# Twelve blocks of the recurrence's output gate, computed for group A only in the shared stage and for group B in its own stage

## The chip, the cores and the metric

The kernel is one launch on one core of one Trainium2 chip. The metric is the device time of that launch in microseconds. All data is fp32, inputs and outputs in HBM.

## What is computed

One decoder layer for 512 prompt tokens and 8 sample tokens. Cut to what matters here:

```
h = rmsnorm(x)
z = h @ w_in              # columns: q 1024, k 1024, v 2048, r 2048, low 16, gu 1024, gv 1024, xq 1024, gates 6144
o = gated linear attention(q, k, v, decay from low)      # 4 heads, d_k 256, d_v 512
branch_a = rmsnorm_per_head(o) * silu(r)                 # r is the recurrence's output gate
branch_b = gMLP spatial gate(gelu(gu), gelu(gv))
branch_c = attention(xq, memory)
merged = g0 * (branch_a @ w_br_gla) + g1 * (branch_b @ w_br_gmlp) + g2 * (branch_c @ w_br_xattn)
x = x + merged @ w_out
x = x + experts(rmsnorm(x))    # product keys, 8 heads, top 16: per token 128 rows of U (dot) and 128 rows of V (sum)
```

## The kernel before, in words

Tokens are split in two groups. **Group A** has prompt tokens 0 to 255 and the 8 samples (264 columns, `WA`), **group B** prompt tokens 256 to 511 (256 columns, `WB`). Features lie on partitions, so a projection is cut in **blocks** of 128 output columns of the weights; a block's weights are one load of 1 MB (`wstream[n]`), and a block is numbered `n` (N_Q, N_K, N_V, N_R, ... are the first blocks of each part of `w_in`; `r` has 16 blocks, N_R to N_R+15).

**The shared stage** (`sp_project`, `act_project`, `dve_project`, `pe_project`) goes through the blocks in order of `n` by the list `PLAIN`, whose last entry is the width: `WA` means that the block is multiplied for A alone, `WZ` for A and B. Here the weights are split on ScalarE (`split_hi`, L531) and VectorE (`split_lo`, L535) in a high and a low part, two slots deep, and each of the 16 pieces of a block is multiplied three times in fp32r (`products`, L551): 48 matmuls of 264 columns for A, 48 more of 256 columns for B. ScalarE evicts with the block's function into `zst2`, SyncE stores the result to `z` (A) and `z_b` (B) in HBM. Before the change all 16 blocks of `r` and all 48 of the gates are `WZ`. Along with the blocks go the samples' steps, at fixed places in `PLAIN`: at N_R ScalarE works out the samples' decay (`act_samples_start`), at N_R+8 PE and ScalarE turn q (`act_samples_q`), and from N_U0 = N_R+12 on each block carries one unit of the samples' state update.

**A's own stages** follow: recurrence, merge of the three branches, w_out, the experts' queries and scores.

**B's passage** (`sp_project_b`, `act_project_b`, `dve_project_b`, `pe_project_b`) then computes the blocks of `PROJECTIONS_B` for B: low, q, k, v, gu, gv, xq, 57 blocks. Weights go to three buffers `raw` in one queue on SyncE (`load_b`, L593; block k+3 is issued when block k is multiplied) and are multiplied unsplit in fp32 (`products_b`, L605, two records a piece, so 32 a block) into two PSUM banks (`bank_b`). ScalarE evicts; most results go through one of four buffers (`z_buffer`, `z_slot`) to `z_b` or `z_late` in HBM. B's recurrence (two chunks of 128 tokens) is woven in: `PE_AT`, `ACT_AT` and `SP_AT` give the passage's block after which an engine does which step, and `dve_project_b` is VectorE's order. Step "r" loads the 16 blocks of `r` from `z_b` into `bra_b`, which VectorE scales by the norm's gain (L1974) and later multiplies by the normalized output (L1947, `o_normed`). Then come `merge_b` for branch a (16 blocks, `bra_b` times w_br_gla), attention, merge for branch c (8 blocks), the spatial gate, merge for branch b (8 blocks), `out_b` (16 blocks of w_out and, after the norm, 16 of the experts' queries, keys and scores) and the **table** stage (`pe_table`, 128 blocks of `peer_u` against B's tokens, L3145). In the merges SyncE's queue alternates weight loads with loads of the gates, and a gate load waits for an eviction by VectorE (`load_gate_b`, L2261).

**The rows.** Beside all of this VectorE works on A's experts: POOL gathers rows (each a 1 MB gather of 128 rows of 8 KB, L2869) into a ring of six, and VectorE takes them one by one: 128 dots with U (L2979), then 128 sums with V (L2984), for two tiles of tokens. The generator `experts_a` holds that order, and `beside(k)` takes k steps of it at fixed places of B's code. It yields ahead of each row, so its call number c works on row c-2. Between rows it also holds the top-16 search of the next tile (`top_head`, eight of them, ahead of V rows 12, 26, 40 ... of the first tile, that is rows 140, 154, 168, 182, 196, 210, 224, 238 over all) and, once the 128 dots are done, `soft_second(0)`, which waits for ScalarE's exponential (`act_soft(0)`); before the change ScalarE does this right after the passage, with the two `act_gelu` of the dots.

## Time and profile before

| what | us |
| --- | --- |
| median of three runs | 4693.71 |
| lowest and highest | 4688.34, 4696.35 |
| span of the profiled execution | 4686.2 |
| PE busy in that span | 4133.9 |
| VectorE busy | 3106.5 |
| GpSimd busy | 1334.0 |
| ScalarE busy | 910.3 |

The profiled execution's own total is not listed beside its span; its span is 7.5 us below the median of the runs and 2.1 us below the lowest, which is what lies around the first and last instruction. PE is TensorE's matmul, PEld its weight load, DVE VectorE, ACT ScalarE, POOL GpSimd, SP SyncE; a name with a q is the engine's issuing side. Stretches are given in us from the start of the span: the shared stage's twelve first blocks of `r` lie at 466.4 to 606.4, B's passage at 1779 to 2281, its merges, attention and spatial gate at 2281 to 2710, `out_b` at 2710 to 2976, the table at 2976 to 3892.

### The profile page before, as it was taken

How to read it: one execution, taken by the hardware profiler on the slowest of the kernel's cores; microseconds unless marked ns; L12 is line 12 of the kernel's file. 1: busy time of each engine (PE TensorE's matmuls, PEld its weight loads, DVE VectorE, ACT ScalarE, POOL GpSimd, SP SyncE). 2: the span in 40 equal slices, each digit the busy share in tenths (PEclk: the TensorE clock that was granted, in tenths of full speed). 3: DMA queues.
4: the chain of work that ended last, by engine and by line, in shares of the span. 5: the costliest groups of instructions: out<-in, count | busy, mean ns of one | idle time of the engine just before them, and what ended most of it. 6: DMA issues, size and time to landing. Idle time of an engine off the chain costs nothing.

```text
span 4686.2 us, 62081 instructions
## 1 busy us (share of the span) xinstructions
PE 4133.9 (88%) x23876; PEld 3601.1 (77%) x23876; DVE 3106.5 (66%) x4549; ACT 910.3 (19%) x1321; POOL 1334.0 (28%) x822
## 2 busy tenths in 40 slices
PE   7999999999898999999876788999999999577555
PEld 7999999999788987887765577887888888344222
DVE  7434134443745656888678876789898457688776
ACT  4334334323432332111000000000000003000100
POOL 0000000000000002444443523444454231466665
PEclk9999999999898999999987798999999999788777
DMA  6555468775354549999999799999999997999998
GB/s 221 199 206 194 146 227 295 284 286 185 117 218 169 211 162 366 417 413 383 418 418 384 312 373 405 423 423 423 418 415 411 404 356 276 413 393 398 422 422 363
DMA packets 304986, 1519.48 MB, mean 324 GB/s; under 512 B 36586, under 2 KB 111802, under 8 KB 138212
## 3 DMA queue, kind: packets, MB, share of 16 engines
q0 software_dynamic: 114288, 830.54, 43.2%
q1 hardware_dynamic: 190500, 686.34, 38.7%
q8 instruction: 119, 1.95, 0.2%
q14 instruction: 79, 0.65, 0.0%
HBM read 1439.05 MB, written 77.71 MB: 324 GB/s over the span
## 4 chain that ended last, share of the span: by engine, by line
PE 59%; DMA 21%; DVE 9%; issue 4%; POOL 3%; DVEq 2%; ACT 2%; ACTq 0%; SPq 0%; POOLq 0%
PE psum L551 30%; PE psum L3145 14%; DMA sb_ring<-in_peer_v,sb_idx_all 8%; PE psum L605 7%; DMA sb_raw<-in_wstream 6%; DMA sb_ring<-in_peer_u,sb_idx_all 3%; POOL sb_ring L2958 2%; PE psum L3401 2%; DVE sb_ring L2979 2%; DVE sb_acc L2984 2%; DMA sb_gt_b<-dram_z_b 1%; PE psum L3383 1%; DVE sb_acc_b L3302 1%; DMA sb_raw_u<-in_wstream 1%; DVEq L2290 1%
## 5 line engine op out<-in xcount | busy, mean ns | idle before, releaser
L551 PE MATMUL psum<-sb_actr,sb_split 128*128 128x264 f32 x8112 | 1005.0, 285 | 27.9 <-DVE sb_actr L2462 12.3
L551 PEld LDWEIGHTS psum<-sb_actr,sb_split 128*128 128x128 f32 x8112 | 993.4, 189 | 33.0 <-issue 22.8
L535 DVE TENSOR_TENSOR sb_split<-sb_raw,sb_split 128x2048 fp32r<-128x2048 f32 x201 | 460.4, 2291 | 698.7 <-ACT sb_split L531 697.7
L2869 POOL DMA_INDIRECT sb_ring<-in_peer_u,sb_idx_all x256 | 421.9, 1648 | 1141.8 <-DVEq L3013 567.0
L2979 DVE CUSTOM_DVE_ANT_0 sb_ring<-sb_ring,sb_htok 128x2048 f32<-128x2048 f32 x264 | 595.4, 2289 | 140.5 <-DMA sb_ring<-in_peer_u,sb_idx_all 134.1
L2984 DVE SCALAR_TENSOR_TENSOR sb_acc<-sb_ring,sb_coef,sb_acc 128x2048 f32<-128x2048 f32 x256 | 601.5, 2350 | 106.5 <-DMA sb_ring<-in_peer_v,sb_idx_all 90.5
L2869 POOL DMA_INDIRECT sb_ring<-in_peer_v,sb_idx_all x256 | 444.6, 1737 | 648.9 <-DVE sb_acc L2984 556.6
L3401 PE MATMUL psum<-sb_ring,sb_diag 128*128 128x512 f32 x512 | 352.8, 853 | 233.2 <-DMA sb_ring<-in_peer_v,sb_idx_all 226.1
L3302 DVE SCALAR_TENSOR_TENSOR sb_acc_b<-sb_ring,sb_coef_b,sb_acc_b 128x2048 f32<-128x2048 f32 x192 | 451.2, 2350 | 131.6 <-DMA sb_ring<-in_peer_v,sb_idx_all 118.5
L2958 POOL DMA_INDIRECT sb_ring<-in_peer_v,sb_idx_all x256 | 435.5, 1701 | 270.2 <-DVE sb_acc_b L3302 132.3
L3401 PEld LDWEIGHTS psum<-sb_ring,sb_diag 128*128 128x128 f32 x512 | 135.3, 277 | 435.0 <-DMA sb_ring<-in_peer_v,sb_idx_all 259.4
L3145 PE MATMUL psum<-sb_h2b,sb_raw_u 128*128 128x256 f32 x2048 | 451.4, 380 | 11.7 <-DMA sb_raw_u<-in_wstream 9.7
L3145 PE MATMUL psum<-sb_h2b,sb_raw 128*128 128x256 f32 x2048 | 450.9, 380 | 9.5 <-DMA sb_raw<-in_wstream 9.4
L3145 PEld LDWEIGHTS psum<-sb_h2b,sb_raw_u 128*128 128x128 f32 x2048 | 387.1, 190 | 72.2 <-DMA sb_raw_u<-in_wstream 18.2
L3145 PEld LDWEIGHTS psum<-sb_h2b,sb_raw 128*128 128x128 f32 x2048 | 387.4, 190 | 69.4 <-DMA sb_raw<-in_wstream 17.5
L531 ACT ACTIVATE sb_split<-sb_raw 128x2048 fp32r<-128x2048 f32 x201 | 384.5, 1913 | 205.9 <-PE psum L551 177.5
L605 PE MATMUL psum<-sb_hxb,sb_raw 128*128 128x256 f32 x1824 | 405.2, 384 | 9.8 <-DMA sb_raw<-in_wstream 7.8
L605 PEld LDWEIGHTS psum<-sb_hxb,sb_raw 128*128 128x128 f32 x1824 | 349.5, 193 | 61.6 <-DMA sb_raw<-in_wstream 10.3
L551 PE MATMUL psum<-sb_actb_hi,sb_split 128*128 128x256 f32 x2048 | 369.0, 279 | 0.0
L551 PEld LDWEIGHTS psum<-sb_actb_hi,sb_split 128*128 128x128 f32 x2048 | 316.3, 188 | 0.0
L551 PE MATMUL psum<-sb_actb_lo,sb_split 128*128 128x256 f32 x1024 | 285.8, 279 | 0.0
L1332 POOL TENSOR_TENSOR sb_kd<-sb_bcum_a 128x1024 f32<-128x1024 f32 x1 | 1.9, 1897 | 728.6 <-DVE sb_att_s L866 728.6
(438 smaller groups left out, 4137.0 us busy)
## 6 DMA issues: line engine op xcount, KB each, us to landing
sb_raw<-in_wstream SPq DMA_DIRECT2D x386, 1024.0 KB
sb_raw_u<-in_wstream SPq DMA_DIRECT2D x64, 1024.0 KB, 18.1
sb_states<-in_state SPq DMA_DIRECT2D x32, 512.0 KB, 3.4
sb_states_t<-in_stateT SPq DMA_DIRECT2D x32, 512.0 KB, 4.0
out_gla_s<-sb_states SPq DMA_DIRECT2D x32, 512.0 KB, 3.1
dram_z<-sb_zst SPq DMA_DIRECT2D x121, 132.0 KB
dram_z_b<-sb_zst SPq DMA_DIRECT2D x77, 128.0 KB
sb_vrow<-dram_v SPq DMA_DIRECT2D x8, 1024.0 KB, 5.0
```

The source lines that it names most:

```text
L531: nc.scalar.activation(split[:, slot, 0, :], raw[:, slot, :], ACT.Copy).then_inc(hi_ready, 1)
L535: nc.vector.tensor_tensor(split[:, slot, 1, :], raw[:, slot, :], split[:, slot, 0, :], ALU.subtract).then_inc(lo_ready, 1)
L551: last = nc.tensor.matmul(psum[:, bank, 0:ntok], w[a], acts(b, kt), start=(i == 0 and a == 0 and b == 0), stop=(i == len(kts) - 1 and a == 1))
L605: last = nc.tensor.matmul(bank_b(q), raw[:, k % 3, w0 + i * P:w0 + (i + 1) * P], acts[:, kt, 0:WB], start=(i == 0), stop=(i == len(kts) - 1))
L2290: dve.drain()
L2869: nc.gpsimd.indirect_dma_start(ring[g % RING][:], None, ins[table], bass.IndirectOffsetOnAxis(ap=col, axis=0)) \
L2958: nc.gpsimd.indirect_dma_start(ring_b[slot_b(y, n)][:], None, ins["peer_v"], bass.IndirectOffsetOnAxis(ap=idx_all[:, 3 + y, n:n + 1], axis ...
L2979: nc.vector.tensor_tensor_reduce(u[:], u[:], htok[:], 1.0, 0.0, ALU.mult, ALU.add, out).then_inc(row_used, 1)
L2984: nc.vector.scalar_tensor_tensor(out=a[:], in0=v[:], scalar=c, in1=a[:], op0=ALU.mult, op1=ALU.add).then_inc(row_used, 1)
L3145: last = nc.tensor.matmul(bank_b(OUTS_U + i), raw_u[u_slot(i)][:, kt * P:(kt + 1) * P], h2b[:, kt, :], start=(kt == 0), stop=(kt == KT - 1))
L3302: nc.vector.scalar_tensor_tensor(out=acc_b[y][:], in0=v[:], scalar=coef_b[y][:, n:n + 1], in1=acc_b[y][:], op0=ALU.mult, op1=ALU.add).then ...
L3401: last = nc.tensor.matmul(psum[:, b, :], diag[:, n // PE_EACH % DIAGS, :], v[:, b * 512:(b + 1) * 512], start=(n < PE_EACH), stop=(n >= SL ...
```

## The change

The first twelve blocks of `r` (N_R to N_J-1, N_J = N_R+12) become `WA` in the shared stage. For B they are loaded and multiplied in the passage, at its places 1 to 12, and evicted with Silu straight into `bra_b`; they are neither stored to `z_b` nor loaded back, and step "r" loads only the last four blocks. Buffers and counters of the stores go by `STORED_B`, the passage's blocks without these twelve. `PE_AT`, `ACT_AT` and `SP_AT` move by 12 (ACT's "ahead_eb" by 2), and ScalarE's `act_soft(0)` and both `act_gelu` move from behind the passage to its place 64 of 0 to 68. VectorE's rows move: 26 to 46 ahead of the first products, 5 to 1 ahead of the last norm, 18 to 24 at the end of the passage; in `out_b` 1 a block instead of 1 and 2 in turn (16 for 24), and 22 for 37 behind the norm. The passage takes 153 calls for 131, `out_b` 44 for 67, which leaves the table one more.

```diff
--- before.py
+++ after.py
@@ -67,7 +67,8 @@
 N_OUT = N_BB + 8
 N_WQ = N_OUT + 16
 N_END = N_WQ + 16
-N_U0 = N_R + 12
+N_J = N_R + 12
+N_U0 = N_J
 N_UNITS = N_U0 + 4 * TS
 N_UEND = N_END + NU
 
@@ -85,18 +86,19 @@
 
 
 OUTS_A = outputs_before(N_END)
-PROJECTIONS_B = (N_LOW,) + tuple(range(N_Q, N_LOW)) + tuple(range(N_GU, N_R)) + tuple(range(N_XQ, N_Q))
+STORED_B = (N_LOW,) + tuple(range(N_Q, N_LOW)) + tuple(range(N_GU, N_R)) + tuple(range(N_XQ, N_Q))
+PROJECTIONS_B = STORED_B[:1] + tuple(range(N_R, N_J)) + STORED_B[1:]
 BLOCKS_B = PROJECTIONS_B + tuple(range(N_BA, N_END))
 
 
 def out_b(n):
 
-    return OUTS_A + (PROJECTIONS_B.index(n) if n < N_R else N_R - N_XQ + outputs_before(n) - N_BA)
+    return OUTS_A + (PROJECTIONS_B.index(n) if n < N_J else len(PROJECTIONS_B) + outputs_before(n) - N_BA)
 
 
 def done_b(n):
 
-    return out_b(n) + 1 if n < N_R else out_b(n + 1)
+    return out_b(n) + 1 if n < N_J else out_b(n + 1)
 
 
 OUTS_U = out_b(N_END)
@@ -608,13 +610,13 @@
 
 
         PLAIN = [(N_MEM0, N_XQ, ACT.Copy, MEM), (N_XQ, N_LOW, ACT.Copy, WA), (N_LOW, N_GU, ACT.Copy, WA),
-                 (N_GU, N_GV, ACT.Gelu, WA), (N_GV, N_R, ACT.Gelu, WA), (N_R, N_R + 4, ACT.Silu, WZ), (N_R + 4, N_R + 8, ACT.Silu, WZ), (N_R + 8, N_U0, ACT.Silu, WZ),
+                 (N_GU, N_GV, ACT.Gelu, WA), (N_GV, N_R, ACT.Gelu, WA), (N_R, N_R + 4, ACT.Silu, WA), (N_R + 4, N_R + 8, ACT.Silu, WA), (N_R + 8, N_J, ACT.Silu, WA),
                  (N_U0, N_G, ACT.Silu, WZ),
                  (N_G, N_UNITS - 4, ACT.Sigmoid, WZ), (N_UNITS - 4, N_UNITS, ACT.Sigmoid, WZ),
                  (N_UNITS, N_BA, ACT.Sigmoid, WZ)]
 
 
-        Z_SINGLE = ((N_R + 1) // 2, N_R // 2)
+        Z_SINGLE = ((N_J + 1) // 2, N_J // 2)
 
         def seg_loop(eng, n0, n1, body):
 
@@ -1235,11 +1237,12 @@
                     pe_samples_turn(pe, 0)
                 if n0 == N_R:
                     pe_samples_turn(pe, 1)
-                    pe.wait_ge(act_lo, 12)
                 if n0 == N_R + 8:
                     pe_samples_q(pe)
                 if n0 == N_U0:
                     pe_samples_own(pe)
+                if n0 == N_J:
+                    pe.wait_ge(act_lo, 12)
                 if n0 == N_UNITS:
                     seg_loop(pe, n0, n0 + ATT_MAX, body)
                     pe_samples_scores(pe)
@@ -1255,9 +1258,9 @@
         Z_A = (N_BA + 1 - Z_SINGLE[0], N_BA - 1 - Z_SINGLE[1], 0, 0)
 
         def z_slot(n):
-            return place_b(n) % 4
-
-        Z_B = tuple(Z_A[k] + len(range(k, N_R - N_XQ, 4)) for k in range(4))
+            return STORED_B.index(n) % 4
+
+        Z_B = tuple(Z_A[k] + len(range(k, len(STORED_B), 4)) for k in range(4))
 
         def z_buffer(n):
 
@@ -1265,7 +1268,7 @@
 
         def z_use_b(n):
 
-            return Z_A[z_slot(n)] + place_b(n) // 4 + 1
+            return Z_A[z_slot(n)] + STORED_B.index(n) // 4 + 1
 
         def func_of(n):
 
@@ -1662,13 +1665,13 @@
 
 
 
-        PE_AT = {3: ("up",), 19: ("sub0", 2), 22: ("sub2", 2), 25: ("sub3", 2), 27: ("kd", 2), 33: ("v", 2), 34: ("o", 2),
-                 35: ("kv", 2), 37: ("sums", 2), 40: ("sub0", 3), 42: ("sub2", 3), 44: ("sub3", 3), 45: ("kd_v", 3), 46: ("o", 3),
-                 47: ("kv", 3), 49: ("sums", 3)}
-        ACT_AT = {5: ("gate",), 10: ("ahead_eb", 2), 20: ("sub2", 2), 23: ("sub3", 2), 28: ("kdtok", 2), 31: ("ahead", 3),
-                  33: ("vtok", 2), 36: ("squares_eb", 2), 38: ("root", 2), 41: ("sub2", 3), 43: ("sub3", 3), 45: ("kdtok_vtok", 3),
-                  48: ("squares", 3), 50: ("root", 3)}
-        SP_AT = {1: ("low",), 4: ("r",), 34: ("q",), 36: ("k",), 39: ("v",), 51: ("state",)}
+        PE_AT = {3: ("up",), 31: ("sub0", 2), 34: ("sub2", 2), 37: ("sub3", 2), 39: ("kd", 2), 45: ("v", 2), 46: ("o", 2),
+                 47: ("kv", 2), 49: ("sums", 2), 52: ("sub0", 3), 54: ("sub2", 3), 56: ("sub3", 3), 57: ("kd_v", 3), 58: ("o", 3),
+                 59: ("kv", 3), 61: ("sums", 3)}
+        ACT_AT = {5: ("gate",), 12: ("ahead_eb", 2), 32: ("sub2", 2), 35: ("sub3", 2), 40: ("kdtok", 2), 43: ("ahead", 3),
+                  45: ("vtok", 2), 48: ("squares_eb", 2), 50: ("root", 2), 53: ("sub2", 3), 55: ("sub3", 3), 57: ("kdtok_vtok", 3),
+                  60: ("squares", 3), 62: ("root", 3), 64: ("soft",)}
+        SP_AT = {1: ("low",), 4: ("r",), 46: ("q",), 48: ("k",), 51: ("v",), 63: ("state",)}
 
         def stored_b(sp, n):
 
@@ -1686,7 +1689,7 @@
             if step == "r":
                 for k in (2, 3):
                     load_gate_b(sp, k)
-                sp.dma_start(bra_b[:], z_b[:, N_R:N_G, :]).then_inc(rc_loaded, 16)
+                sp.dma_start(bra_b[:, N_J - N_R:KT, :], z_b[:, N_J:N_G, :]).then_inc(rc_loaded, 16)
             if step == "q":
                 stored_b(sp, 33)
                 sp.wait_ge(sub_ready, 12)
@@ -1709,8 +1712,11 @@
         def sp_project_b(sp):
             for k, n in enumerate(PROJECTIONS_B):
                 load_b(sp, k + 3)
-                sp.wait_ge(evac_done, out_b(n) + 1)
-                if N_Q <= n < N_LOW:
+                if n in STORED_B:
+                    sp.wait_ge(evac_done, out_b(n) + 1)
+                if N_R <= n < N_J:
+                    pass
+                elif N_Q <= n < N_LOW:
                     sp.dma_start(z_late[:, n - N_Q, :], z_buffer(n)[:, CH:WB]).then_inc(z_stored[z_slot(n)], 16)
                 else:
                     sp.dma_start(z_b[:, n, :], z_buffer(n)).then_inc(z_stored[z_slot(n)], 16)
@@ -1842,6 +1848,10 @@
                 act.wait_ge(kv_ready, 8 * c + 8)
                 nc.scalar.activation(vc_b[:].rearrange("p (h j) t -> p h (j t)", h=4), psum[:, 0:4, :],
                                      ACT.Square).then_inc(squares_ready, 1)
+            if step == "soft":
+                act_soft(act, 0)
+                act_gelu(act, 0)
+                act_gelu(act, 1)
             if step == "root":
                 act.wait_ge(root_in, ROOTS_GLA[1] + c + 2)
                 nc.scalar.activation(norm_b[:], norm_b[:], ACT.Sqrt).then_inc(root_out, 1)
@@ -1855,11 +1865,13 @@
         def act_project_b(act):
             for k, n in enumerate(PROJECTIONS_B):
                 act.wait_ge(out_ready, out_b(n) + 1)
-                if z_use_b(n) > 1:
+                if n in STORED_B and z_use_b(n) > 1:
                     act.wait_ge(z_stored[z_slot(n)], 16 * (z_use_b(n) - 1))
                 if N_Q <= n < N_LOW:
                     nc.scalar.activation(chunk_of(n), bank_b(out_b(n))[:, 0:CH], ACT.Copy)
                     nc.scalar.activation(z_buffer(n)[:, CH:WB], bank_b(out_b(n))[:, CH:WB], ACT.Copy).then_inc(evac_done, 1)
+                elif N_R <= n < N_J:
+                    nc.scalar.activation(bra_b[:, n - N_R, :], bank_b(out_b(n)), ACT.Silu).then_inc(evac_done, 1)
                 else:
                     nc.scalar.activation(z_buffer(n), bank_b(out_b(n)), func_of(n)).then_inc(evac_done, 1)
                 if k in ACT_AT:
@@ -1967,9 +1979,10 @@
             sub_exponents(2, 0)
             sub_exponents(2, 1)
             kd_exponents(2)
-            beside(26)
+            beside(46)
             products_ahead(2)
             dve.wait_ge(rc_loaded, 48)
+            dve.wait_ge(evac_done, out_b(N_J - 1) + 1)
             for kt in range(KT):
                 nc.vector.tensor_scalar(bra_b[:, kt, :], bra_b[:, kt, :], pcols[:, C_GLA + kt:C_GLA + kt + 1], None, ALU.mult)
             beside(4)
@@ -1987,9 +2000,9 @@
             scores(3, (2, 2, 2, 2))
             beside(13)
             new_state(3)
-            beside(5)
+            beside(1)
             normed_out(3)
-            beside(18)
+            beside(24)
 
 
 
@@ -2266,7 +2279,7 @@
                 if n == N_BC + 2:
                     sp.dma_start(x1b[:], ins["xbT"]).then_inc(x1_loaded, 16)
                 if n == N_BA:
-                    stored_b(sp, N_R - N_XQ)
+                    stored_b(sp, len(STORED_B))
                     for k in (0, 1):
                         load_gate_b(sp, k)
                 if n == N_BA + 3:
@@ -2709,7 +2722,7 @@
             nc.vector.memset(ssum[:], 0.0)
             dve.drain()
             for n in range(N_OUT, N_WQ):
-                beside(1 + n % 2)
+                beside(1)
                 dve.wait_ge(out_ready, out_b(n + 1))
                 at = x1b[:, n - N_OUT, :]
                 nc.vector.tensor_tensor(at, bank_b(out_b(n)), at, ALU.add).then_inc(evac_done, 1)
@@ -2729,7 +2742,7 @@
                                                       scalar=pcols[:, C_FFN + kt:C_FFN + kt + 1],
                                                       in1=rstd[:, 0:WB], op0=ALU.mult, op1=ALU.mult)
             dve.drain().then_inc(normed, 1)
-            beside(37)
+            beside(22)
 
         def pe_out_b(pe):
             pe.wait_ge(merged_ready, 5)
@@ -3475,9 +3488,6 @@
             act_merge(act, N_BB, N_OUT)
             act_out(act)
             act_project_b(act)
-            act_soft(act, 0)
-            act_gelu(act, 0)
-            act_gelu(act, 1)
             act_attention(act, GB)
             act_spatial(act, GB)
             act_out_b(act)
```

## Rows read from the trace of the kernel before

**Rows 1.** The page: the span, and the busy time of each engine

```profile
span 4686.2 us, 62081 instructions
PE 4133.9 (88%) x23876; PEld 3601.1 (77%) x23876; DVE 3106.5 (66%) x4549; ACT 910.3 (19%) x1321; POOL 1334.0 (28%) x822
```

**Rows 2.** Stretches: length, busy us (instructions) by engine, PE clock, DMA share, GB/s

```profile
466.40:606.40 140.00, 139.31 (x1174) 138.74 (x1172) 28.00 (x15) 42.16 (x48) 0.41 (x2) 1.00 0.41 147
1779.00:2281.00 502.00, 473.19 (x2304) 406.55 (x2304) 400.79 (x585) 69.10 (x137) 200.91 (x126) 0.96 0.99 406
2281.00:2438.00 157.00, 118.43 (x512) 100.41 (x512) 115.52 (x138) 4.73 (x7) 73.79 (x41) 0.87 1.01 418
...
2710.00:2823.00 113.00, 112.12 (x512) 98.09 (x512) 83.12 (x110) 0.00 (x0) 34.54 (x26) 0.99 0.94 371
...
2848.00:2962.00 114.00, 110.60 (x493) 96.28 (x493) 70.46 (x60) 5.75 (x15) 41.05 (x31) 0.96 1.00 412
2976.00:3892.00 916.00, 895.88 (x4101) 775.21 (x4102) 702.00 (x1196) 65.66 (x270) 384.52 (x231) 1.00 1.00 409
```

**Rows 3.** PE in order of time, shared stage: start, us, what, idle before

```profile
385.80 11.87 PE L551 MATMUL psum<-sb_actr,sb_split 128*128 128x264 f32 x96 [1.92 <-ACT sb_zst L1042]
...
478.83 6.06 PE L551 MATMUL psum<-sb_actr,sb_split 128*128 128x264 f32 x48 [0.69 <-DVE sb_split L535]
484.73 0.28 PE L551 MATMUL psum<-sb_actb_hi,sb_split 128*128 128x256 f32 x1
...
490.33 5.97 PE L551 MATMUL psum<-sb_actr,sb_split 128*128 128x264 f32 x48
496.14 0.28 PE L551 MATMUL psum<-sb_actb_hi,sb_split 128*128 128x256 f32 x1
```

**Rows 4.** ScalarE in order of time, at the first block of r

```profile
471.19 1.28 ACT L705 ACT_TABLE_LOAD   x1
472.48 0.26 ACT L705 ACTIVATE sb_es<-sb_gxs 128x64 f32<-128x64 f32 x1
...
474.34 1.92 ACT L531 ACTIVATE sb_split<-sb_raw 128x2048 fp32r<-128x2048 f32 x1
```

**Rows 5.** PE in order of time, B's passage

```profile
1849.30 85.00 PE L605 MATMUL psum<-sb_hxb,sb_raw 128*128 128x256 f32 x384 [5.82 <-DMA sb_raw<-in_wstream]
```

**Rows 6.** DMA issues in B's passage: KB each, median us to landing

```profile
sb_bra_b<-dram_z_b SPq DMA_DIRECT2D x1, 2048.0 KB, 23.7
```

**Rows 7.** VectorE in order of time, end of the passage and first merge

```profile
2240.49 3.35 DVE L1941 RECIPROCAL sb_norm_b<-sb_norm_b 128x512 f32<-128x512 f32 x1 [3.71 <-ACT sb_norm_b L1847]
...
2259.57 2.28 DVE L2979 CUSTOM_DVE_ANT_0 sb_ring<-sb_ring,sb_htok 128x2048 f32<-128x2048 f32 x1
...
2302.31 2.29 DVE L2979 CUSTOM_DVE_ANT_0 sb_ring<-sb_ring,sb_htok 128x2048 f32<-128x2048 f32 x1 [2.32 <-DMA sb_ring<-in_peer_u,sb_idx_all]
...
2315.82 0.41 DVE L2288 TENSOR_TENSOR sb_merged<-psum,sb_gt 128x256 f32<-128x256 f32 x1
```

**Rows 8.** ScalarE in order of time, end of the passage

```profile
2251.94 0.38 ACT L1864 ACTIVATE sb_zst<-psum 128x256 f32<-128x256 f32 x1 [6.52 <-PE psum L605]
...
2282.37 0.31 ACT L2847 ACTIVATE sb_gate_all<-sb_gate_all 128x128 f32<-128x128 f32 x1
```

**Rows 9.** PE in order of time: waits in B's merges, attention and spatial gate

```profile
2328.23 23.88 PE L605 MATMUL psum<-sb_bra_b,sb_raw 128*128 128x256 f32 x96 [16.71 <-DMA sb_raw<-in_wstream]
...
2473.80 1.12 PE L2061 MATMUL psum<-sb_ident,sb_prob 128*128 128x128 f32 x4 [6.66 <-DVE sb_prob L2133]
...
2605.76 0.80 PE L2351 MATMUL psum<-sb_wspat,sb_vn 128*128 128x128 f32 x2 [10.63 <-DVE sb_vn L2420]
```

**Rows 10.** PE's waits from 2847 to 3900: us in total, times, longest

```profile
PE psum L3145 <- DMA sb_raw_u<-in_wstream: 9.7, 20, 1.4
PE psum L3145 <- DMA sb_raw<-in_wstream: 9.4, 19, 1.4
...
PE psum L605 <- DMA sb_raw<-in_wstream: 3.4, 1, 3.4
```

## The prediction

> **What bounds the kernel now.** I read the page first: PE is busy for 4133.9 of 4686.2 us, VectorE for 3106.5 [rows 1]. Such shares mix stages, so next came the stretches [rows 2]. The reader is to see three regimes. In the shared stage at the first twelve blocks of r, PE is busy for 139.31 of 140.00 us while the transfers move only 147 GB/s: PE alone sets the pace. In B's passage both are full: PE 473.19 of 502.00 us, DMA share 0.99. In the first merge PE has 118.43 of 157.00 and the DMA share is 1.01: transfers, and VectorE's place in them, set the pace. From 2710 on PE leads again: 512 records, which are 16 blocks, in 112.12 of 113.00 us, so 7.0 us a block, and the table's 128 blocks take 916, of which 895.88 are PE. The waits of PE in those last stages come to 9.7, 9.4 and 3.4 us [rows 10].
>
> Durations are from the one profiled execution with its span of 4686.2; the median of the runs, 4693.71, is 7.5 higher, and I add my difference to the median.
>
> **What is taken out of the shared stage.** In order of time [rows 3] B's part of a block runs from 484.73 to 490.33, 5.60 us, and A's from 490.33 to 496.14, 5.81. Twelve of B's parts are 67.2 us. Three things give some back, as a block now covers 5.8 us and not 11.4.
> - At the first block of r ScalarE works out the samples' decay, and its split of the second block starts only at 474.34 [rows 4]. It takes 1.92, VectorE's lower part follows, and PE starts at 478.83 after a wait of 0.69 [rows 3]. B's part of the first block hid this: that block's A part ended one B part (5.60) and the wait earlier, at about 472.5. Without the B part PE waits from there to 478.83, 6.4 for 0.69: 5.8 lost.
> - ScalarE changes its function table around the segments' first blocks. In the A-only segment ahead of r such places cost PE up to 1.92 us each [rows 3]. For three segments I take 3.3; bounds 0 and 6.
> - The turning of the samples' q at the ninth block delays the next split. No row of an A-only block has it; between 0 and 2, I take 1.
> VectorE's and SyncE's work per block fits: A-only blocks ran at 5.8 in the stretch before. The stores of z_b that go (twelve of 128 KB) cost nothing at 147 GB/s and bring nothing. Sum: 67.2 - 5.8 - 3.3 - 1 = **57 us gained**, bounds 51 and 62.
> One table load lasts 1.28 us here and the activation behind it starts 0.01 us after [rows 4]. The Trainium skill (ScalarE: Activation LUTs, What ACT_TABLE_LOAD costs) counts a drain of about 1.38 us more per switch, 2.66 together. By that rule some six switches would cost an estimated 8 us more and the gain would be 49; the row speaks for the load alone, and the sum goes by the row.
>
> **What is put into the passage.** 384 records, twelve blocks, took 85.00 us beside full transfers [rows 5]; so the twelve new blocks are 85.0 us of PE. Unsplit fp32 costs 7.08 us a block where the split product cost 5.60: on PE the exchange alone loses 18 us. By bytes: 12 weight loads of 1.049 MB are 12.6 MB, 22 more gathered rows 23.1, and the load of bra_b shrinks from 2048 to 512 KB [rows 6], -1.6. At the 418 GB/s of a full stretch [rows 2] the 34.1 MB take 81.6 us. So both limits grow alike, and 22 rows are about what the time can carry. The smaller bra_b load takes 3.8 us off a crowded moment in which PE waited 5.82 for weights [rows 5]; I take all of it: **81 us lost**, bounds 76 and 88. ScalarE's eviction into bra_b, one piece less on SyncE's queue (no store) and the scaling by VectorE, which waits for an eviction long done, are on no path: the twelve blocks are the first of the passage.
>
> **The backlog at the first merge.** VectorE ends the passage late already: its rows run on to 2302.31 and its first merge eviction is at 2315.82 [rows 7], while PE was done with the passage at 2281; PE waits 16.71 for weights [rows 9] whose issue stands behind that eviction on SyncE's queue. The change adds here. First, six more rows at the end: between 2259.57 and 2302.31 ten rows took 42.7, 4.3 each, so 26 us with weights flowing, or 15 at 418 GB/s once PE stands and they don't. Second, a wait: call 129 now falls inside the last norm, and it ends in soft_second(0), which needs ScalarE's exponential. That moves to place 64, three blocks behind the sums; its eviction is at 2251.94 in the old times, the exponential about 2 us later, where the reciprocal began at 2240.49 [rows 7, 8]. VectorE would stand some 15 us, its ring full and POOL behind it. SyncE, PE and ScalarE go on; PE needs the norm's result only at 2281. Together 30 to 41 us of later rows, cushioned by faster gathers while PE stands, by fuller buffers afterwards, and by the exponential and the gelus that before came at 2282.37. I take **20 us lost**, bounds 0 and 40.
>
> **The searches move.** With 22 more rows behind it, each later stage meets other top-16 searches. By the calls, attention has one before (row 168) and none after; PE waited 6.66 there. The spatial gate has one (196) and none after; PE waited 10.63 [rows 9]. The first merge gets three for two, the second two for one. Attention and spatial gate are chains of small steps, so 7 and 9 are gained; in the merges about 5 are given back: **11 gained**, bounds 0 and 18.
>
> **What out_b and the table gain.** They lose 23 - 1 rows of 1 MB, 23 MB, which would be 55 us by transfers. But PE bounds these blocks at 7.0 us, and all its waits for weights there are 22.5 [rows 10]. VectorE doesn't hold PE up in them. The 6 rows inside the norm stay. I take **6 gained**, bounds 0 and 22. The end of the kernel is untouched.
>
> **Sum:** -57 + 81 + 20 - 11 - 6 = +27, so 4694 + 27 = **4721**. About 0.2% (9.4 us) is what a measurement of this kernel can tell from no change.
>
> **The rivals.**
> - *Bytes set the end of B's part* (faster). If the transfers bound everything from 1779 to 3892, rows taken out of out_b pay for those put into the passage, and only 12.6 - 1.6 = 11.0 MB are new: 26 us. Then -57 + 26 = -31: 4663. It decides if PE's 85 us find idle PE time later. For it: DMA shares of 0.99 to 1.01 from 1779 to 2438, and 1.00 in the table. Against: in the stage that the rows leave, PE is busy 112.12 of 113.00 at 371 GB/s, and nothing there can become shorter.
> The Trainium skill (DMA: Bandwidth & Descriptors, Issuing engines are not separate DMA queues) says that transfers from all issuing engines interleave on the same 16 DMA engines. That rule makes gathers and weights one account, as this rival has it.
> - *A draw.* The backlog is swallowed by buffers and the late stages save most of their waits: -57 + 81 + 3 - 11 - 16 = 0: 4694.
> - *The backlog compounds* (slower still). VectorE comes 40 us late to the first merge, three searches there instead of two add 9, nothing is saved later: -57 + 84 + 40 - 11 - 0 = +56: 4750. It decides if the stand for the exponential and the six rows add up in full at 2281.
> - *The change doesn't do what it says*: compiled code keeps the pace of the shared stage, because ScalarE and VectorE can't follow at 5.8 us. The A-only rows speak against it; then +30 on top.
>
> **Chances.** Forecast with its spread 0.45, compounding 0.15, draw 0.17, bytes 0.20, the last 0.03. Of the forecast's 0.45 some 0.03 falls below no change. Faster by over 0.2%: 0.21; within: 0.15; slower: 0.64. The forecast's own range is 4700 to 4745; the range with the rivals that carry eight in ten is 4668 to 4750.
>
> **What would show it.** In the profile after: the first twelve blocks of r in 80 to 86 us; 12 x 32 more records of L605 and a passage of about 583 us with PE busy near 94%; L2837 in VectorE's waits with some 15 us for ScalarE ahead of L1941; PE's first long wait of the merges longer by some 20; no search inside attention and spatial gate; out_b's 16 blocks still in 112 us, the table in 905 to 916. It is wrong if out_b and table shrink by more than 22 us together, or if the first merge isn't later than the passage's end by more than before.

## The result: 0.74% slower, and the profile after

The kernel after takes 4727.59 us (median of four runs, 4722.02 to 4734.17) where the kernel before took 4695.03 on the same chip: ratio 1.0074, 95% interval [1.0061, 1.0086]. The forecast was 4721, slower, with 4668 to 4750. The profiled execution spans 4720.1 us for 4686.2, +33.9.

The page after, span and busy time (it answers to [rows 1]):

```profile
span 4720.1 us, 61688 instructions
PE 4136.6 (88%) x23684; PEld 3601.0 (76%) x23684; DVE 3106.9 (66%) x4549; ACT 914.8 (19%) x1323; POOL 1332.4 (28%) x822
```

PE's busy time is 2.7 us more than before in total, so nearly all of the 33.9 us that were lost is waiting. The shares show no more; the stretches do (columns as in [rows 2]):

```profile
468.80:550.20 81.40, 74.17 (x596) 73.19 (x594) 28.00 (x15) 39.31 (x37) 0.38 (x2) 0.96 0.62 220
1719.00:2291.00 572.00, 553.06 (x2686) 474.75 (x2687) 431.05 (x608) 79.24 (x155) 208.60 (x139) 0.98 0.98 402
2291.00:2489.00 198.00, 118.63 (x515) 101.33 (x514) 153.70 (x209) 1.67 (x2) 92.84 (x50) 0.80 0.95 388
2749.00:2863.00 114.00, 113.42 (x512) 99.17 (x512) 55.74 (x70) 0.00 (x0) 16.52 (x18) 0.97 0.89 333
3012.00:3926.00 914.00, 897.81 (x4141) 780.81 (x4140) 689.46 (x1184) 70.45 (x275) 389.99 (x225) 1.00 0.97 398
```

The reader is to see one row above all: the first merge, 198 us for the same 118 us of PE work that took 157 before. In `out_b` the transfers fell from 371 to 333 GB/s and the stretch still has its 114 us.

The lengths of the stages, each from PE's first instruction of the stage to its first of the next, in us. For e9 to e12 see the experiments:

| stage | before | after | e9 | e10 | e12 |
| --- | --- | --- | --- | --- | --- |
| shared and A's stages | 1779.3 | 1719.1 | 1789.5 | 1724.7 | 1718.4 |
| B's passage | 501.9 | 572.4 | 563.9 | 563.6 | 569.7 |
| first merge | 157.1 | 198.1 | 197.4 | 159.6 | 136.3 |
| attention | 41.7 | 37.8 | 34.5 | 41.7 | 41.7 |
| second merge | 88.1 | 90.6 | 90.6 | 85.4 | 88.9 |
| spatial gate | 51.6 | 42.3 | 42.3 | 51.6 | 51.6 |
| third merge | 90.0 | 89.3 | 87.9 | 90.7 | 90.1 |
| `out_b`, both halves | 266.5 | 266.9 | 265.1 | 267.9 | 267.6 |
| table | 917.9 | 908.6 | 910.5 | 915.7 | 915.5 |
| end | 792.0 | 795.1 | 791.4 | 788.4 | 792.6 |

PE at the first blocks of r (it answers to [rows 3]): the wait of 6.28 us, where the forecast had 6.4.

```profile
468.83 6.06 PE L553 MATMUL psum<-sb_actr,sb_split 128*128 128x264 f32 x48
481.16 9.01 PE L553 MATMUL psum<-sb_actr,sb_split 128*128 128x264 f32 x57 [6.28 <-DVE sb_split L537]
```

The end of the passage and the first merge of after, in order of time, on VectorE (it answers to [rows 7]):

```profile
2266.14 0.28 DVE L2850 TENSOR_REDUCE sb_sums<-sb_gate_all 128x8 f32<-128x128 f32 x1 [17.72 <-ACT sb_gate_all L2860]
...
2267.16 3.35 DVE L1953 RECIPROCAL sb_norm_b<-sb_norm_b 128x512 f32<-128x512 f32 x1
...
2311.99 0.48 DVE L2789 MAX8 sb_top_v<-sb_sc 128x8 f32<-128x128 f32 x2
...
2321.69 34.27 DVE L2997 SCALAR_TENSOR_TENSOR sb_acc<-sb_ring,sb_coef,sb_acc 128x2048 f32<-128x2048 f32 x14
2355.88 0.41 DVE L2301 TENSOR_TENSOR sb_merged<-psum,sb_gt 128x256 f32<-128x256 f32 x1
2356.22 0.48 DVE L2789 MAX8 sb_top_v<-sb_sc 128x8 f32<-128x128 f32 x2
...
2474.71 0.48 DVE L2789 MAX8 sb_top_v<-sb_sc 128x8 f32<-128x128 f32 x2
...
2489.10 0.42 DVE L2301 TENSOR_TENSOR sb_merged<-psum,sb_gt_b 128x256 f32<-128x256 f32 x1
```

on ScalarE (to [rows 8]):

```profile
2264.03 0.38 ACT L1876 ACTIVATE sb_zst<-psum 128x256 f32<-128x256 f32 x1 [6.52 <-PE psum L607]
2264.43 1.28 ACT L2860 ACT_TABLE_LOAD   x1
2265.73 0.31 ACT L2860 ACTIVATE sb_gate_all<-sb_gate_all 128x128 f32<-128x128 f32 x1
```

on SyncE's queue, where the row of 51.26 us is three loads of gates, the third issued at its end:

```profile
2305.39 51.26 SPq L2274 DMA_DIRECT2D sb_gt<-dram_z_b  x3
2356.70 0.45 SPq L595 DMA_DIRECT2D sb_raw<-in_wstream  x1
```

and on PE (to [rows 9]):

```profile
2291.46 27.79 PE L607 MATMUL psum<-sb_bra_b,sb_raw 128*128 128x256 f32 x128
2367.39 9.87 PE L607 MATMUL psum<-sb_bra_b,sb_raw 128*128 128x256 f32 x32 [48.14 <-DMA sb_raw<-in_wstream]
...
2489.57 6.76 PE L2037 MATMUL psum<-sb_kvt,sb_xq 128*128 128x256 f32 x16 [11.36 <-DVE sb_merged L2301]
```

This is one chain. VectorE stands 17.72 us for the exponential, so the reciprocal starts at 2267.16. The rows behind it, and one top-16 search (the first MAX8, at 2311.99, until the rows go on at 2321.69), run to 2355.88, which is 64.4 us behind PE's first instruction of the merge (34.6 before). SyncE's third gate load waits for that first eviction; the next weight load is issued at 2356.70, the moment it is free, and PE gets it after 48.14 us of waiting. PE's row names the weights, but these were not slow: they landed within 10.7 us of their issue (PE goes on at 2367.39). They were issued late. At the merge's end another search, at 2474.71, stands ahead of the last eviction, and PE waits 11.36 us for it at the start of the attention. Before, that wait was 0.88:

```profile
2438.35 3.72 PE L2024 MATMUL psum<-sb_kvt,sb_xq 128*128 128x256 f32 x16 [0.88 <-DVE sb_merged L2288]
```

The late waits (answer to [rows 10]), PE from 2890 to 3930:

```profile
PE psum L3158 <- DMA sb_raw<-in_wstream: 6.9, 15, 1.4
PE psum L3158 <- DMA sb_raw_u<-in_wstream: 6.1, 13, 1.4
PE psum L607 <- DMA sb_raw<-in_wstream: 4.3, 1, 4.3
```

### The profile page after: what moved, and what is told of

It is laid out like the page before. It is cut to its first block, busy times and chain, and to the rows that moved or that the text cites. A ratio compares the mean times of both kernels' runs of the same rounds, so it can differ in the third digit from the quotient of the medians.

```text
span 4720.1 us, 61688 instructions
## 1 busy us (share of the span) xinstructions
PE 4136.6 (88%) x23684; PEld 3601.0 (76%) x23684; DVE 3106.9 (66%) x4549; ACT 914.8 (19%) x1323; POOL 1332.4 (28%) x822
## 4 chain that ended last, share of the span: by engine, by line
PE 61%; DMA 19%; DVE 9%; issue 5%; POOL 3%; DVEq 2%; ACT 2%; SPq 0%; ACTq 0%; POOLq 0%
PE psum L553 28%; PE psum L3158 15%; PE psum L607 11%; DMA sb_ring<-in_peer_v,sb_idx_all 9%; DMA sb_raw<-in_wstream 8%; DVE sb_acc L2997 2%; POOL sb_ring L2971 2%; DVE sb_acc_b L3315 1%; PE psum L3414 1%; PE psum L3396 1%; DVE sb_ring L2992 1%; DMA sb_raw_u<-in_wstream 1%; DVEq L2303 1%; DVE sb_split L537 1%; POOL sb_ring L2882 1%
## 5 line engine op out<-in xcount | busy, mean ns | idle before, releaser
L2882 POOL DMA_INDIRECT sb_ring<-in_peer_u,sb_idx_all x256 | 393.1, 1536 | 1257.8 <-DVE sb_dots L2992 586.8
L2882 POOL DMA_INDIRECT sb_ring<-in_peer_v,sb_idx_all x256 | 473.8, 1851 | 617.6 <-DVE sb_acc L2997 525.5
L2971 POOL DMA_INDIRECT sb_ring<-in_peer_v,sb_idx_all x256 | 433.5, 1693 | 273.8 <-DVE sb_acc_b L3315 139.1
L607 PE MATMUL psum<-sb_hxb,sb_raw 128*128 128x256 f32 x2208 | 490.5, 383 | 12.6 <-DMA sb_raw<-in_wstream 10.6
L607 PEld LDWEIGHTS psum<-sb_hxb,sb_raw 128*128 128x128 f32 x2208 | 420.9, 192 | 78.3 <-DMA sb_raw<-in_wstream 17.7
L553 PE MATMUL psum<-sb_actb_hi,sb_split 128*128 128x256 f32 x1664 | 299.8, 279 | 0.0
L553 PEld LDWEIGHTS psum<-sb_actb_hi,sb_split 128*128 128x128 f32 x1664 | 257.0, 188 | 0.0
L553 PE MATMUL psum<-sb_actb_lo,sb_split 128*128 128x256 f32 x832 | 232.2, 279 | 0.0
L3114 ACT ACTIVATE sb_a_tile<-psum 128x128 f32<-128x128 f32 x128 | 35.5, 278 | 840.3 <-PE psum L3158 840.3
```

The source lines that it names most:

```text
L553: last = nc.tensor.matmul(psum[:, bank, 0:ntok], w[a], acts(b, kt), start=(i == 0 and a == 0 and b == 0), stop=(i == len(kts) - 1 and a == 1))
L607: last = nc.tensor.matmul(bank_b(q), raw[:, k % 3, w0 + i * P:w0 + (i + 1) * P], acts[:, kt, 0:WB], start=(i == 0), stop=(i == len(kts) - 1))
L2882: nc.gpsimd.indirect_dma_start(ring[g % RING][:], None, ins[table], bass.IndirectOffsetOnAxis(ap=col, axis=0)) \
L2971: nc.gpsimd.indirect_dma_start(ring_b[slot_b(y, n)][:], None, ins["peer_v"], bass.IndirectOffsetOnAxis(ap=idx_all[:, 3 + y, n:n + 1], axis ...
```

## The experiments

Twelve kernels ran; ratios are to the kernel before, run alongside. The theory ("by code") was that the passage pays PE's price for the twelve blocks and that VectorE's lateness at the first merge pays for the rest. Against it stood bytes as one account over all of B's stages.

**e1 to e3: the lateness, piece by piece.**

e1 is the kernel after, with the exponential before the norm's root and the gelus left at place 64:

```diff
-                  60: ("squares", 3), 62: ("root", 3), 64: ("soft",)}
+                  60: ("squares", 3), 61: ("exp",), 62: ("root", 3), 64: ("gelus",)}
...
-            if step == "soft":
+            if step == "exp":
                 act_soft(act, 0)
+            if step == "gelus":
                 act_gelu(act, 0)
```

> The changed kernel, but ScalarE works out the exponential for soft_second(0) at place 61 of the passage; only the two gelus stay at place 64. My theory (VectorE stands 17.7 us inside the last norm for an exponential three blocks too late, and arrives at the first merge that much later): VectorE's wait at the sum of the softmax shrinks to 2 to 5 us, the first merge eviction moves from 64 us behind the passage's end to 50 to 54, and the kernel gains 8 to 16 us against the changed kernel, so 4712 to 4720 where the kernel before is at 4695. Rival (the end of this part is set by the bytes that the transfers have to move, so a stand of VectorE is made good by gathers that land meanwhile): within 4 us of the changed kernel, 4724 to 4731.

4718.25, ratio 1.0063 [1.0050, 1.0076]: about 5 us gained on after by the ratios, so little that the intervals leave it open. By the ratio this is missed: the kernel before ran at 4688.06 beside it and not at 4695, and 1.0063 is where the rival's 4724 to 4731 lay. The merge still took 192.8, and its first eviction came 58.3 us behind PE and not 50 to 54. VectorE's reciprocal starts 14.6 us earlier, but then VectorE stands 5.3 us for the gelus, and 10.7 us for gathers where it had stood 7.6. So taking the stand away brings the eviction 6.1 us forward and not 14.6: the gelus are what VectorE would have waited for next.

e2 is the kernel after, six rows moved from the end of the passage behind the norm:

```diff
-            beside(24)
+            beside(18)
...
-            beside(22)
+            beside(28)
```

> The changed kernel, but 18 rows instead of 24 at the end of the passage and 28 instead of 22 behind the norm of out_b. My theory (the six rows are backlog at the first merge, and out_b and table are bound by PE, so the rows are nearly free there): the first merge eviction comes 14 to 20 us earlier, the merges gain that, out_b and table lose 0 to 3; 4710 to 4716. Rival (bytes set the end of B's part): the same bytes in another order, 4724 to 4731.

4710.75, ratio 1.0046 [1.0032, 1.0060], about 13 us gained, as expected; the merge fell to 169.9. Its first eviction came 14.6 us earlier, which is the time of six rows. The edit does a second thing: no search stands ahead of the merge's last eviction any more, and PE waits 1.22 us there and not 11.36; the attention has one instead (44.5 us for 37.8). The table did not grow (906.8), as the six rows fell in `out_b`, with 56 gathers there for 49.

e3 is the kernel after, twenty rows moved from ahead of the first products behind the norm:

```diff
-            beside(46)
+            beside(26)
...
-            beside(22)
+            beside(42)
```

> The changed kernel, but 26 rows as before instead of 46 ahead of the first products, and 42 instead of 22 behind out_b's norm: the rows' move is undone, the move of the twelve blocks stays. My theory (the passage is bound by PE, with or without the 20 rows; the late stages are bound by PE and have room for some 27 rows): passage 565 to 572 us instead of 572, out_b and table 3 to 8 longer, the searches fall on other stages again (one in attention, one in the spatial gate: 7 and 9 us lost there, some given back in the merges); 4727 to 4742. Rival (bytes set the pace): the passage is 20 x 2.5 = 50 us of transfers lighter and out_b and table 50 us heavier, so the passage drops to PE's 553 and the late stages grow by 30 or more; 4745 to 4760.

4732.10, ratio 1.0092 [1.0078, 1.0106]. The number is inside the first expectation, its terms are not: the first merge fell from 198.1 to 138.2, but the passage grew to 607.0 (565 to 572 expected) and the table by 23 to 931.6 (3 to 8 expected with `out_b`). The passage grew by an accident of the edit. With 20 calls fewer ahead, the dot of row 127 falls behind the norm, and ScalarE, which takes the gelus at place 64, waits 49.67 us for it and evicts nothing. ScalarE of e3 in order of time:

```profile
2316.63 0.26 ACT L2984 ACTIVATE sb_gelus<-sb_dots 128x64 f32<-128x64 f32 x1 [49.67 <-DVEq L3042]
```

and PE of e3, held up by it:

```profile
2317.30 12.93 PE L607 MATMUL psum<-sb_hxb,sb_raw 128*128 128x256 f32 x49 [40.14 <-ACT sb_zst L1876]
```

So e3 says nothing of the rows in the passage. It does show that with twenty calls fewer ahead, place 64 is too early for the gelus.

**e4: PE's work without bytes.** The kernel before, the passage's places 1 to 12 multiplied twice from the same weights.

```diff
-            for i, kt in enumerate(kts):
+            for i, kt in list(enumerate(kts)) * (2 if 1 <= k <= 12 else 1):
```

> The kernel before, but in B's passage the blocks at places 1 to 12 are multiplied twice from the same loaded weights: 84 us more of PE, no byte and no row more. My theory (PE sets the passage, the backlog of VectorE's rows sets the first merge): passage 502 + 84 less 10 to 20 of waits that PE has for VectorE and weights, so 566 to 576; VectorE comes to the passage's end with more rows landed, but its order of rows is fixed, so the first merge stays within 10 us of its 157; total 4755 to 4770. Rival (bytes set the whole of B's part, the transfers are full for most of it): PE's second pass fills time in which the transfers catch up, and later stages get shorter by most of it; total under 4730.

4743.23, ratio 1.0115 [1.0098, 1.0132]; the passage +57.4, the first merge unchanged (155.9). The stretch:

```profile
1780.00:2339.00 559.00, 547.85 (x2688) 475.48 (x2688) 400.95 (x586) 68.89 (x137) 208.07 (x127) 0.98 0.91 365
```

PE work alone lengthens the passage while the transfers relax to 365 GB/s. That is against the bytes rival. But the 384 records more, 79.1 us by their busy time (484.3 for 405.2), made the passage only 57.4 longer: less than the 64 to 74 of the first expectation, and a total between the two. It is the first sign that the passage had idle PE time to give.

**e5 and e6: both repairs, and more of one.** e5 is e1 and e2 together; e6 has `beside(8)` at the end of the passage and `beside(38)` behind the norm.

> The changed kernel with both edits: the exponential at place 61, and 18 rows at the passage's end with 28 behind out_b's norm. My theory (the backlog at the first merge is the sum of the stand for the exponential and of the rows): the two gains of their own runs, 5 and 13 us against the changed kernel, add up, so about 18 less than the changed kernel, ratio to the kernel before 1.0025 to 1.0050; the passage and first merge together 735 to 742 us where the changed kernel has 770. Rival (bytes): no more than the better of the two, ratio 1.0045 or above.

4702.35, ratio 1.0021 [1.0012, 1.0030], some 25 us off after, just more than the first expectation had (1.0025 to 1.0050), and the rival is out; merge 159.8, table 909.5. What happens at the first merge was the change's largest loss, and together the two repairs took no less off than the sum of their own (18). As in e2, a search leaves the merge for the attention with them.

> The changed kernel with the exponential at place 61 and only 8 rows at the passage's end, 38 behind out_b's norm. My theory: the backlog is gone, PE waits at the first merge no longer than its transfers need (50 MB of weights and rows and 4 MB of others at 418 GB/s, some 130 to 140 us for the merge), out_b and table take the rows for 0 to 5 us; 40 to 60 us less than the changed kernel, ratio 0.994 to 0.999. Rival (bytes set the whole of B's part): moved rows bring nothing beyond the stand for the exponential, ratio 1.004 or above.

4701.11, ratio 1.0015 [1.0006, 1.0024]: missed, between the two expectations, with 28 us off after and not 40 to 60. The merge fell further, to 145.4, but against e5 the second merge took 7 more and the table 922.1, 12.6 more, with seven rows more in it.

**e7 and e8: the same on the kernel before.** e7 has 8 for 18 rows at the passage's end and 47 for 37 behind the norm; e8 also 8 fewer in the first merge (`beside(1 + n % 2)` there) and 55.

> The kernel before, its blocks as they are, but with 8 rows instead of 18 at the passage's end and 47 instead of 37 behind out_b's norm. My theory (the backlog was there before the change, smaller): first merge 157 falls to 130 to 138, the spatial gate loses its search (9 us), out_b and table take the ten rows for 0 to 10; ratio 0.991 to 0.996, and 10 to 20 us below the changed kernel with the same treatment (PE: 12 blocks cost 7.0 us in the passage for 5.6 in the shared stage). Rival (bytes): ratio 0.999 to 1.001.

4708.15, ratio 1.0029 [1.0020, 1.0038]: missed in its sign, and above the rival too. The merge fell by 16.6 and the spatial gate by 9, but the table took 942.6, 24.7 more. PE's waits there (e7, from 2970):

```profile
PE psum L3145 <- DMA sb_raw_u<-in_wstream: 18.3, 35, 1.4
PE psum L3145 <- DMA sb_raw<-in_wstream: 17.4, 35, 1.4
```

35.7 for 19.1 in [rows 10]. Ten rows of 1.05 MB at the 418 GB/s of [rows 2] are 25 us: in the kernel before, PE and the transfers are both full in the table, and each of these rows costs its bytes.

> As the one before, and the first merge takes 1 and 2 rows in turn instead of 2 a block, with 55 behind out_b's norm. My theory: a block of the first merge then needs 2.8 MB, 6.6 us of transfers, less than PE's 7.0, so the merge falls to 115 to 122; but the late stages have room for about 15 rows and get 18, so they lose 5 to 15; ratio 0.988 to 0.996. Rival (bytes): ratio 0.999 to 1.001.

4689.76, ratio 0.9992 [0.9982, 1.0001]: no difference from before, and missed; merge 133 where 115 to 122 were expected, table 960, 42 more where 5 to 15 were expected for all late stages. The number is the rival's, but the stages moved, and in total they gave back what the merge gained.

**e9 and e10: the change in two halves.** e9 is the kernel before with the change's rows and its place for `act_soft`, without the blocks:

```diff
-            beside(26)
+            beside(46)
...
-            beside(5)
+            beside(1)
             normed_out(3)
-            beside(18)
+            beside(24)
...
-                beside(1 + n % 2)
+                beside(1)
...
-            beside(37)
+            beside(22)
```

> The kernel before with the change's rows alone: 46 calls for 26 ahead of the first products, 1 for 5 and 24 for 18 around the last norm, 1 a block in out_b, 22 for 37 behind the norm, and act_soft with both gelus at the passage's place 52 of 0 to 56. The twelve blocks of r stay where they were. 'By code' (what 'after' now shows): the passage was bounded by the transfers at 0.99, so 22 rows of 1.05 MB cost it about 23.1 / 0.418 = 55 us, less what its idle PE does not give, say +45 to +60; the first merge +35 to +45 as in 'after' (same rows and the same stand for the exponential at its end); searches -11, table -5 to -20: +60 to +80, ratio 1.013 to 1.017. If bytes are one account over all stages of B, rows that move pay for themselves: passage and merge +90, out and table -60 to -80, ratio 1.002 to 1.006.

4767.87, ratio 1.0163 [1.0147, 1.0179]. The number is inside the first expectation, the reason is not the one given. PE in the passage of e9:

```profile
2010.54 3.07 PE L1735 MATMUL psum<-sb_qi_b,sb_ki_b 128*32 128x32 f32 x32 [64.38 <-DVEq L1896]
```

Without the blocks PE wants the recurrence's operands at place 19 and not 31, and 46 rows lie ahead of them: PE stands 64.38 us for VectorE, at a DMA share of 0.95. So e9's passage (+62) gives no price of bytes. Its first merge does say something: 197.4, as in after. The merge's loss is made by the rows, with the searches among them, and the exponential, and the blocks have no part in it. Its first eviction comes at 63.6 us and PE's wait for the last is 11.18.

e10 is the kernel after with all rows, `act_soft` and the gelus placed as in the kernel before: the twelve blocks alone.

> The kernel after with its rows put back where they were before (26, 5, 18, 1 and 2 a block in out_b, 37), act_soft and the gelus behind the passage: the twelve blocks alone. On PE the passage needs 12 x 7.0 = 84 more than the 473 it was busy, 557; by bytes 11 MB more than the 502 us full before, +26. 'By code': A -60, the passage is the larger of 557 plus a few us and 528, so +57 to +65 (as e4_pe_twice, +57, which had the PE work and no bytes), the first merge as before (0 to +5), later stages as before or up to +10 slower since nothing is taken from them: -3 to +15 in all, ratio 0.999 to 1.003. Rival (bytes decide in the passage and after): the passage +26 to +40 and the total -20 to -35, ratio 0.993 to 0.996. If the change of rows in 'after' was what cost the time, this kernel is at most as long as the one before.

4699.23, ratio 1.0017 [1.0008, 1.0026], the top half of "by code"; the rival's 0.993 to 0.996 is out. A -54.6, the passage +61.7, the first merge +2.5. And the passage leaves something unused, VectorE in e10:

```profile
1938.92 0.43 DVE L1900 SCALAR_TENSOR_TENSOR sb_qi_b<-sb_qi_b,sb_qc_b 128x256 f32<-128x256 f32 x1 [54.37 <-ACT sb_zst L1872]
...
2325.08 0.42 DVE L2301 TENSOR_TENSOR sb_merged<-psum,sb_gt 128x256 f32<-128x256 f32 x1
```

VectorE stands 54.37 us for k and q, twelve blocks later than before, and is then 36.8 us late at the merge (2325.08 against PE's start there at 2288.3).

**e11: fewer rows in the first merge of e5.** 8 fewer, 36 behind the norm.

> The kernel after with the exponential at place 61, 18 rows at the end of the passage and 8 fewer in the first merge (1 and 2 in turn), 36 behind the norm for 22. e5 (without the last edit) was at 1.0021; its first merge took 160 where 128 us are what the late stages' pace would give. If eight rows less shorten that merge as they did from e7 to e8 (-7) with the attention's wait gone (-9) and the late stages have room for them: -8 to -20 against e5, ratio 0.998 to 1.0005. Rival: the late stages are full too (e7's table +25 for ten rows): the merge's gain is given back and the ratio stays at 1.001 to 1.003.

4697.22, ratio 1.0008 [0.9998, 1.0018]. The merge took 158.8, as in e5, attention 34.7 for 44.5, the table 915.3 for 909.5. Some 6 us off e5 by the ratios, less than the 8 to 20 of the first expectation and between the two: the attention gave what was expected, the merge nothing, and the table took a part. It is no better than before.

**e12: e10 with fourteen rows moved from the end of the passage into VectorE's 54 us.**

```diff
-            beside(26)
+            beside(40)
             products_ahead(2)
...
             normed_out(3)
-            beside(18)
+            beside(4)
```

> e10_blocks_alone with fourteen of its rows moved within the passage: 40 calls for 26 ahead of the first products, 4 for 18 at the end; the passage keeps its 131 calls and its bytes. In e10's trace VectorE stands 54.4 us in one piece before the first products of chunk 2, with DMA share 0.81 from 1865 to 2005, and is late at the first merge by its last rows. If the idle of VectorE in the middle and its lateness at the end are one and the same 14 rows: they fill the 54 us (about 4 us a row at the bytes' pace), the passage stays at 560 to 566, the first merge falls from 159.6 by what its late start and full ring cost, to 120 to 140 (e6, with 16 fewer, was at 145 and e8 at 133), later stages as in e10: -20 to -40, ratio 0.993 to 0.998, ahead of both kernels. Rival: the first merge is bound by its own 40 odd rows, three or two searches and its gates at DMA share 1.01, whatever VectorE brings along from the passage: -0 to -8, ratio 1.000 to 1.002; or what is gained there is given back in the table, as in e7 (but no row goes there).

4680.27, ratio 0.9980 [0.9971, 0.9989]: ahead of before and of after, and 17 us off e10 by the ratios, just short of the 20 to 40 expected. It has the same rows and bytes as e10, and VectorE's first eviction lies 13.9 us behind PE's start of the merge at 2288.1:

```profile
2290.47 0.28 DVE L2850 TENSOR_REDUCE sb_sums<-sb_gate_all 128x8 f32<-128x128 f32 x1 [29.07 <-ACT sb_gate_all L2860]
...
2301.97 0.42 DVE L2301 TENSOR_TENSOR sb_merged<-psum,sb_gt 128x256 f32<-128x256 f32 x1
```

The merge took 136.3, inside the 120 to 140 expected, the passage 569.7, 6 us more than e10's and above the 560 to 566 (between it and the table nothing moved by more than 4). VectorE now stands 29.07 us for the exponential, behind the passage's end; bringing that forward as e1 did is the next step, and it wasn't tried.

## Why the prediction was right, and which terms were off

The change was to cost 27 us and cost 34 by the spans, 33 by the medians. That this is so near is luck in part: the passage came 10.5 us cheaper than forecast and the first merge 21 dearer, and the two errors have different causes. The terms, in their order:

- **Out of the shared stage, -57 forecast, -60.2 measured**, inside 51 to 62. The twelve blocks took 81.4 us for 140.0. Of the three deductions only the decay's wait is seen by itself (6.28). By the drain that the Trainium skill (ScalarE: Activation LUTs, What ACT_TABLE_LOAD costs) adds to each switch the gain would have been an estimated 49. The trace doesn't agree: the stretch gave 58.6, and at the exponential the load of 1.28 us starts 0.02 us behind the eviction ahead of it and is followed within 0.02 us.
- **Into the passage, +81 forecast, +70.5 measured**, below the bound of 76. PE's work came out as said: 85.0 us in [rows 5] for 384 records, and the passage's records of this kind went from 405.2 to 490.0 us. PE's groups by form in the passage of before:

```profile
L605 PE MATMUL psum<-sb_hxb,sb_raw 128*128 128x256 f32 x1824 | 405.2, 384 | 9.8 <-DMA sb_raw<-in_wstream 7.8 <-ACT sb_stage L2507 2.0
```

and of after:

```profile
L607 PE MATMUL psum<-sb_hxb,sb_raw 128*128 128x256 f32 x2206 | 490.0, 383 | 12.6 <-DMA sb_raw<-in_wstream 10.6 <-ACT sb_stage L2520 2.0
```

What I had not counted was the 28.8 us of the passage in which PE did nothing (502.00 less 473.19 in [rows 2]), of which I counted on 3.8. The recurrence's operands, made by VectorE and ScalarE, had held PE up 10.7 and 8.4 us; with twelve more blocks ahead of them it was 6.5 and 1.6. That is 11 us. PE's waits in the passage of before:

```profile
PE psum L1789 <- DVE sb_state L1931: 10.7, 2, 6.8
PE psum L1735 <- DVEq L1892: 8.4, 3, 4.7
```

and of after:

```profile
PE psum L1795 <- DVE sb_state L1943: 6.5, 1, 6.5
...
PE psum L1741 <- DVEq L1904: 1.6, 1, 1.6
```

The recurrence's own PE steps took 63.1 for 68.0 (553.06 less 490.0, 473.19 less 405.2). e4 shows the same without any change of bytes. "So both limits grow alike" was not so. The passage moved 229.9 MB (402 GB/s for 572 us) for 203.8 (406 for 502), 26 MB more and not 34.1, which are 62 us at 418 GB/s. Of the 22 rows written into it GpSimd gathered only 13 more while PE was in the passage (137 for 124); the other nine were gathered in the first merge (49 for 40), as VectorE runs behind PE there.
- **The backlog at the first merge, +20 forecast, +41.0 measured**, just above the bound of 40. The chain was as told: the stand for the exponential (15 forecast, 17.72 measured), the six rows behind it, the eviction on which the gate load hangs. PE's last product of the merge came 30.5 us later (186.8 us into the stage for 156.3), and the wait for the last eviction was 10.5 longer (11.36 for 0.88). The 30.5 are, within a microsecond, what the first eviction was later, 29.8. These split up as follows. The reciprocal starts 16.4 us later against PE (24.3 us ahead of the merge for 40.7). From there to the first eviction VectorE does 26 rows for 20, 15.1 us of work more. Its waits for gathers in that time (from 2240.4 to 2315.9 before, from 2267 to 2356 after) shrink by 12.1, before:

```profile
DVE sb_ring L2979 <- DMA sb_ring<-in_peer_u,sb_idx_all: 19.7, 10, 5.4
```

and after:

```profile
DVE sb_acc L2997 <- DMA sb_ring<-in_peer_v,sb_idx_all: 7.6, 4, 3.6
```

One search adds 9.7, and 0.7 are left over. So the backlog as I meant it, stand and rows less the cushion of faster gathers, is 16.4 + 15.1 - 12.1 = 19.4 us, and the 20 for it were right, cushion and all. e2 bears out the rows: without the six the first eviction comes 14.6 us earlier. The stand is worth less by itself, 6.1 us in e1. The search directly behind the first eviction puts the second one 14.4 us behind it (5.0 before), which the merge makes good by its end.
- **The searches, -11 forecast.** This is the term that was mis-sized. Attention -3.9, the spatial gate -9.3, the second and third merge +2.5 and -0.7 are the -11.4 that I had for all of it; the 10.63 of [rows 9] is a wait of 1.32. But I priced the searches that come to the merges at about 5 together, and two of them stand where nothing covers them: the one among the rows at the passage's end, ahead of the first eviction (9.7), and the one ahead of the last eviction (10.5). With these 20 the searches cost about 9 us and gained none. Over the kernels traced the merge takes what its first eviction is late, plus 109 to 123 where no search stands ahead of the last eviction: 157.1 at 34.6 (before), 159.8 at 42.8 (e5), 159.6 at 36.8 (e10), 136.3 at 13.9 (e12). It is plus 134 to 135 in the three kernels that have one there: 198.1 at 64.4 (after), 192.8 at 58.3 (e1), 197.4 at 63.6 (e9). No run moves a search alone; in e2 and e5 it goes together with the six rows.
- **`out_b` and the table, -6 forecast.** +0.4 and -9.3, and the untouched end +3.1, which moves by that much among kernels with the same end. The claim that nothing shrinks where PE is busy 112.12 of 113.00 held: `out_b` lost sixteen gathers (49 for 65) and kept its length. The table lost six (212 for 218) and got 9.3 shorter.

**The rivals.** The bytes rival is out for the change: e10 has its 11 MB and shows its passage at +61.7 and not +26. In the table it comes near: ten rows more cost 24.7 us (e7) and 21 more cost 42 (e8), six fewer gave 9.3 (after), so 1.6 to 2.5 us a row where the bytes alone would be 2.5. In `out_b` it fails. The compounding rival had the right price for the merge (40) for another reason, the stand and the rows in full; half of it is searches, and the passage and the late stages gave where it had nothing. The draw would have needed the merge at +3; e5, which mends the merge (+2.7), is nearly that (1.0021). The change does what it says: 81.4 us for the twelve blocks.

**What the difference is made of.** By the spans the blocks alone cost 3.1 (e10), and the rows on top of them 30.8. The profiled execution of e10 was its fastest of twelve; by the ratios of the medians it is 8 and 27. The 30.8 are: first merge 38.5, passage 8.8, less 9.4 from the attention to the third merge and 8.1 in `out_b` and the table, with 1.1 net in the first stage and the end. This holds for this order alone: on the kernel before the same rows cost 76 us (e9). I had costed the row moves as filling what the blocks open. The harm is done at the first merge, by the six rows at the end, the searches that the moved rows bring there and, for some 5 us (e1), the call for the exponential inside the norm.

## What to carry to other kernels

When work moves into a stage, its length there is the bounding engine's time less that engine's idle time that now gets covered: take the idle apart by what it waits for. When filler work moves along, put it where the helper engine begins to stand (VectorE's 54 us ahead of the products) and not at the end of a stage whose successor hangs on the same engine. And place filler work by when the helper does it, not by the stage it is written in: look for its dearest step (here a search of 9.7 us) ahead of the first and the last hand-over of a stage, where nothing covers it.

## What the runs showed of the hardware that was not expected

The granted clock of PE, a mean over the stretch with 1.00 for full speed, was 0.96 in the twelve A-only blocks, where it had been 1.00 with twice the work per block ([rows 2]), and PE was busy 74.17 of 81.40 us in them. In the passage it went the other way, from 0.96 to 0.98, as PE's idle time shrank, and in the first merge it was 0.80, 0.87 and 0.92 with 60, 75 and 84% busy (after, before, e12). The same blocks kept PE busy for 118.63, 118.43 and 113.94 us there, so the lower clock goes with at most 4.7 us more of work. The stretch of e12:

```profile
2288.10:2424.40 136.30, 113.94 (x514) 98.77 (x512) 102.13 (x126) 4.94 (x7) 66.47 (x34) 0.92 0.97 396
```
